# Router and expert stages joined into one block, norm rows loaded earlier, norm done in place, value read moved to the end

## The chip, the cores and the metric

The kernel runs on one core of a Trainium2 chip, as one program. The metric is the device time of one execution in microseconds, as the median over runs; smaller is better. The profile shows one execution of it, with the engines PE (TensorE), DVE (VectorE), ACT (ScalarE), POOL (GpSimd) and SP (SyncE), which only issues transfers here.

## The reference, cut to what matters

A sequence of 256 tokens of width 1024 goes through two layers of one transformer (attention mixers and a feed-forward net), and then through a second block, of which the end matters here: a layer norm, a router and 16 experts.

```python
def layer_norm(x, g, b):
    mu = jnp.mean(x, -1); var = jnp.mean(jnp.square(x - mu), -1)
    return (x - mu) * lax.rsqrt(var + LN_EPS) * g + b
...
# second block, after the mixer has added its output to x:
x = layer_norm(x, ln1_g, ln1_b)
scores = sigmoid(x @ w_router)                      # 16 experts, 4 groups of 4
biased = scores + router_bias
# of each group the best sum of two biased scores; the best group is kept;
# in it the two best experts; their scores, divided by their sum, are weights
x = ALPHA * x + sum over the chosen experts of
        weight * ((silu(x @ w_gate[e]) * (x @ w_up[e])) @ w_down[e])
return layer_norm(x, ln2_g, ln2_b)
```

(The lines under the dots are a summary in words of this text's own; the norm is the reference's, shortened.) Each token goes to two experts of one group.

## The kernel before, in words

Everything is in float32 precision. A float32 product is made of three products of a faster 32-bit form: the operand is split into a high part (ACT copies it, `Ring.hi`, L172) and a low part (DVE subtracts the high part from it, `Ring.lo`, L184), and PE multiplies high by high, high by low and low by high.

**Weights** come in units of 1 MB through a `Ring`: SP issues a unit's transfer (`Ring.feed`, L159) as soon as the raw slot of the unit five places earlier has been split by DVE; ACT and DVE split it into one of 4 pairs; PE multiplies by it and counts it as used, which lets ACT split the unit four places later. An expert has six units: two for the gate, two for the up product, two for the down product.

**Blocks.** The program is a row of blocks (`nc.Block()`): inside one, each engine has its own list of instructions, and the lists meet through semaphores only. At a block's end every engine stops until all are there. Around the change the order of blocks is:

1. `project("mixer_out", ...)` (L2782): the output products of the mixer, added to `x` by DVE (L2779). All its weight units are issued in the block before. Then `clear_semaphores` (L3516), a block of its own.
2. `normalize_and_route` (L2207, its block starts at L2225). SP issues the two norm rows (L2229, 512 KB each), router weights and bias (L2230, L2231), and the first five expert units. DVE sums `x` (L2166), then waits for the rows (`dve.wait_ge(*loaded)`), writes `(x - mean) * gain` into a work tile (L2170) and `work * rstd + bias` back into `x` (L2175). ACT squares (L2154) and POOL takes the inverse root (L259, L260) beside that. PE transposes `x` (L2244); ACT and DVE bring it to `hT` (L2274, L2299) and split `x` into the pair `x_pair` (L2276, L2302); PE multiplies by the router weights (L2254); ACT takes the sigmoid (L2279); DVE then works alone through small instructions of some 0.2 us, one waiting for the other: the group of each token (L2306 to L2318), then, after PE has counted the tokens of each group (L2259 to L2263), the slot of each token (`slot_key`, L2321), the **gather table** `G` of ones and zeros in eight instructions (L2325), the largest group (L2327), and the two experts' weights, `combine` (L2289 to L2337) and `combine_rest` (L2339).
3. `nc.values_load` (L2118): every engine reads the size of the largest group into a register.
4. `sparse_experts` (L2342, block at L2373). PE multiplies `x_pair` by the gather table, 16 pieces `n` of two 128x512 products (L2433), which sorts the tokens by group; the pieces go through 7 PSUM banks, and the even ones are taken out by ACT (L2475), the odd ones by DVE (L2477), two copies of 128x256 each. After pieces 2, 5, 10 and 13 PE turns one group's table (L2441) and gathers its weights (L2443), and ACT takes both out (L2492, L2493) after its pieces 2, 6, 10 and 14. ACT and DVE make the splits of units 0 to 3 between the pieces: unit 0 first of all, then one after ACT's pieces 4, 8, 12 and DVE's 5, 9, 13. When all is out, the experts run, 0 to 15: gate (L2385), turn of the expert before (L2396), up (L2385), down of the expert before (L2409), and after each fourth one the scatter back to tokens (L2423).
5. `nc.If(n_most > P)` (L2120 on): a dense path for the case in which a group has over 128 tokens. It isn't taken. Then `last_norm` with its own rows and work tile, and the result is stored.

`TileNorm` (L2143) is used by steps 2 and 5.

```python
PICK = (3, 6, 7, 4, 5, 0, 1)                      # banks of the gather's pieces
...
ring.lo(dve, 0)
for n in range(1, 16, 2):
    dve.wait_ge(picked, n + 1)
    picked_out(n)
    if n in (5, 9, 13):
        ring.lo(dve, n // 4)
```

## Time and profile before

| | |
|---|---|
| median of 3 runs | 1820.74 us (1813.05, 1820.74, 1821.1) |
| the profiled execution | 1813.24 us, of which the span of the trace is 1811.3 us |
| PE busy | 1604.7 us, 89% of the span |
| DVE busy | 1227.2 us, 68% |
| ACT busy | 816.4 us, 45% |
| moved by DMA | 348.07 MB, mean 192 GB/s |

Times in the rows are microseconds from the span's start. A row of the timeline gives start, length, engine, line and operation, how many instructions stand in it (x2: two, one behind the other), and in brackets the idle time ahead of it with what ended it. "PEq" and the like is the sequencer of an engine, which handles waits, branches and register loads.

### The profile page before, as it was taken

Reading aid. Unit: us, or ns where it says so; the run is one execution under the profiler, and the core shown is the slowest. Engines: PE = TensorE matmul, PEld = TensorE weight load, DVE = VectorE, ACT = ScalarE, POOL = GpSimd, SP = SyncE. Lnnn points to the kernel's source line nnn. Section 1 sums busy time; section 2 is a strip of 40 time slices with the busy share of each in tenths; the row PEclk is TensorE's granted clock in tenths of the full one; section 3 lists DMA queues with packets and bytes.
Section 4 is the critical chain, followed back from the end, with each engine's and each line's share of the span. In section 5 each row is a group of like instructions: output and inputs, shape, how many; then the busy total and the mean of one; then the engine's idle time right before and its main releaser. Section 6 shows DMA issues by size and latency. Waiting matters only on the chain. (4 is left out here: it accounts for less than half of the span.)

```text
span 1811.3 us, 25509 instructions
## 1 busy us (share of the span) xinstructions
PE 1604.7 (89%) x10701; PEld 1449.5 (80%) x10701; DVE 1227.2 (68%) x1354; ACT 816.4 (45%) x943; POOL 42.4 (2%) x60
## 2 busy tenths in 40 slices
PE   2899998999899998999969997897798958999995
PEld 2789887999798988899958997886686857888884
DVE  4877586988757557665554875534575757899895
ACT  1345533434344553443323662225433327777773
POOL 0100000000100000000000000000000000000000
PEclk9999999999999999999979998987887969999998
DMA  8975446999844324666245553111222447999992
GB/s 302 318 231 163 140 140 189 351 324 328 251 147 134 108 89 147 218 228 214 93 156 178 157 169 93 47 47 47 79 85 71 139 142 255 374 349 366 365 345 106
DMA packets 226057, 348.07 MB, mean 192 GB/s; under 512 B 14612, under 2 KB 156672, under 8 KB 225808
## 3 DMA queue, kind: packets, MB, share of 16 engines
q1 hardware_dynamic: 225936, 346.36, 57.1%
q8 instruction: 87, 1.43, 0.3%
q14 instruction: 34, 0.28, 0.1%
HBM read 345.29 MB, written 1.97 MB: 192 GB/s over the span
## 5 line engine op out<-in xcount | busy, mean ns | idle before, releaser
L459 PE MATMUL bank<-layer_split,hT_pair 128*128 128x256 f32 (+2 forms) x4032 | 512.7, 287 | 31.3 <-DVE hT_pair L1031 21.6
L459 PEld LDWEIGHTS bank<-layer_split,hT_pair 128*128 128x128 f32 x4032 | 486.2, 190 | 45.2 <-issue 29.9
L184 DVE TENSOR_TENSOR layer_split<-layer_raw,layer_split 128x2048 fp32r<-128x2048 f32 x122 | 279.6, 2292 | 100.8 <-ACT layer_split L172 99.4
L172 ACT ACTIVATE layer_split<-layer_raw 128x2048 fp32r<-128x2048 f32 x122 | 233.5, 1914 | 195.1 <-PE bank L459 73.7
L184 DVE TENSOR_TENSOR expert_split<-expert_raw,expert_split 128x2048 fp32r<-128x2048 f32 x96 | 219.5, 2290 | 40.7 <-ACT expert_split L172 40.6
L172 ACT ACTIVATE expert_split<-expert_raw 128x2048 fp32r<-128x2048 f32 x96 | 184.2, 1920 | 76.2 <-PE bank L2385 39.3
L459 PE MATMUL bank<-split_w,hT_pair 128*128 128x256 f32 (+1 forms) x1248 | 180.8, 308 | 13.6 <-PEq L2580 5.0
L459 PEld LDWEIGHTS bank<-split_w,hT_pair 128*128 128x128 f32 x1248 | 170.5, 204 | 24.3 <-issue 18.7
L184 DVE TENSOR_TENSOR split_w<-raw_w,split_w 128x2048 fp32r<-128x2048 f32 x52 | 119.2, 2293 | 66.2 <-ACT split_w L172 65.6
L1894 PE MATMUL bank<-layer_split,ffnh_aT 128*128 128x512 f32 x528 | 127.0, 396 | 2.8 <-DVE ffnh_aT L1962 2.8
L172 ACT ACTIVATE split_w<-raw_w 128x2048 fp32r<-128x2048 f32 x52 | 99.4, 1912 | 59.2 <-PE bank L459 50.7
L459 PE MATMUL bank<-hT_pair,split_w 128*128 128x256 f32 x960 | 120.7, 288 | 4.1 <-DVE hT_pair L315 4.0
L459 PEld LDWEIGHTS bank<-hT_pair,split_w 128*128 128x128 f32 x960 | 118.3, 193 | 5.7 <-issue 5.2
L1894 PEld LDWEIGHTS bank<-layer_split,ffnh_aT 128*128 128x128 f32 x528 | 98.0, 188 | 25.8 <-DVE ffnh_aT L1962 3.3
L2385 PE MATMUL bank<-expert_split,hT_pair 128*128 128x512 f32 x384 | 93.6, 401 | 4.2 <-DVE gathered_pair L2477 4.2
L2409 PE MATMUL bank<-expert_split,expert_hidden_T 128*128 128x512 f32 x384 | 91.3, 394 | 1.4 <-DVE expert_hidden_T L2543 1.4
L2385 PE MATMUL bank<-expert_split,gathered_pair 128*128 128x512 f32 x384 | 92.6, 396 | 0.0
L2385 PEld LDWEIGHTS bank<-expert_split,hT_pair 128*128 128x128 f32 x384 | 72.7, 191 | 21.2 <-issue 4.6
L2409 PEld LDWEIGHTS bank<-expert_split,expert_hidden_T 128*128 128x128 f32 x384 | 72.2, 188 | 18.0 <-DVE expert_hidden_T L2543 1.6
L2385 PEld LDWEIGHTS bank<-expert_split,gathered_pair 128*128 128x128 f32 x384 | 71.6, 188 | 16.3
L204 DVE SCALAR_TENSOR_TENSOR ada_acc<-layer_raw,silu_c,ada_acc 128x1024 f32<-128x1024 f32 x40 | 51.7, 1294 | 1.4
L459 PE MATMUL bank<-layer_split,merge_pair 128*128 128x256 f32 x384 | 47.8, 284 | 0.4 <-DVE merge_pair L1765 0.4
(455 smaller groups left out, 1756.4 us busy)
## 6 DMA issues: line engine op xcount, KB each, us to landing
layer_raw<-in_ada_w SPq DMA_DIRECT2D x48, 1024.0 KB, 6.9
layer_raw<-in_ffn_w_gate_up SPq DMA_DIRECT2D x44, 1024.0 KB, 5.6
raw_w<-in_w_in SPq DMA_DIRECT2D x40, 1024.0 KB, 5.1
layer_raw<-in_w_in SPq DMA_DIRECT2D x38, 1024.0 KB, 6.1
expert_raw<-in_w_gate SPq DMA_DIRECT2D x32, 1024.0 KB, 7.1
expert_raw<-in_w_up SPq DMA_DIRECT2D x32, 1024.0 KB, 7.2
expert_raw<-in_w_down SPq DMA_DIRECT2D x32, 1024.0 KB, 6.9
layer_raw<-in_ffn_w_down SPq DMA_DIRECT2D x22, 1024.0 KB, 5.4
```

What stands on the lines that cost most here:

```text
L172: self.nc.scalar.activation(self.pair[:, j % self.pairs, 0, 0:self.size[n]], self.raw[:, n % self.depth, 0:self.size[n]], ACT.Copy).then_i ...
L184: self.nc.vector.tensor_tensor(self.pair[:, j % self.pairs, 1, 0:self.size[n]], self.raw[:, n % self.depth, 0:self.size[n]], self.pair[:, ...
L204: self.nc.vector.scalar_tensor_tensor(acc[:, :], second, self.scale[:, 2 * q + 1:2 * q + 2], acc[:, :], ALU.mult, ALU.add).then_inc(self.l ...
L459: ins = nc.tensor.matmul(out, lhs, rhs, start=first and c == chunks[0] and tp + wp == 0, stop=last and c == chunks[-1] and tp == 1)
L1894: ins = nc.tensor.matmul(ps[4 + 2 * t + nb][:, :], self.aT[:, tp, c, t * P:(t + 1) * P], w[:, c, nb * 512:(nb + 1) * 512], start=n == 0 an ...
L2385: ins = nc.tensor.matmul(ps[bank][:, :], gathered[e // PER // 2][:, tp, 4 * i + c, slot_cut(e // PER)], ring.view(u + i, wp, 4, 512)[:, c, :],
L2409: ins = nc.tensor.matmul(ps[OUT_BANKS[nb]][:, :], aT[:, tp, 2 * i + c, :], ring.view(u + i, wp, 2, D)[:, c, nb * 512:(nb + 1) * 512], star ...
```

## The change

- The route step is no block of its own. `normalize_and_route` becomes `routing`, which returns four lists (tensor, scalar, vector, gpsimd), and `sparse_experts` becomes `routed_experts`, which puts them at the front of its own engines' lists, in its block.
- PE's gather waits for a semaphore `g_ready` of the eight table instructions. The weights `combine` have another, `combined`, which PE waits for ahead of the first table turned. The maximum (`most`) moves ahead of the slot key.
- The order in the gather changes: banks, who takes which piece out (ACT 9, DVE 7), where the tables stand (after pieces 6, 8, 10, 13), and the splits of units 0 to 3: ACT makes the high parts of 0, 1 and 2 behind the router's sigmoids and 3 behind the gather; DVE makes the low part of 0 while PE counts, 1 behind piece 7, and 2 and 3 behind the gather.
- Norm rows, router weights and bias are issued at the end of SP's list in the `mixer_out` block. The rows lie in `hT`, which is free there.
- The first norm writes `(x - mean) * gain` into `x` itself, and so waits for ACT's square of that tile first. The second norm keeps its work tile.
- `values_load` stands behind the experts' block, right ahead of the `If`.

```diff
+            def load_rows(sp):
+                rows, w, bias = ln_rows[0:3]
+                for i, name in enumerate(("ln1_g_2", "ln1_b_2")):
+                    sp.dma_start(rows[:, i, :], A[name].broadcast_to([P, D])).then_inc(rows_in, 16)
...
-                    normalize_and_route(ring, comb, member, key, rest, most, most_int, xP, G)
-                    n_most = nc.values_load(most_int[0:1, 0:1], min_val=0, max_val=S)
-                    sparse_experts(ring, comb, xP, G, s1)
+                    scratch = sb("silu_hidden", [P, D], s1)
+                    g_ready, combined = new_sem(nc, "route_tables_out"), Count(nc, "route_combined")
+                    route = routing(ring, comb, member, key, rest, most, most_int, xP, G, s1, ln_rows, scratch, g_ready, combined)
+                    routed_experts(ring, comb, xP, G, s1, scratch, route, g_ready, combined)
+                n_most = nc.values_load(most_int[0:1, 0:1], min_val=0, max_val=S)
...
                 dve.wait_ge(*loaded)
+                centred = x if self.in_place else self.work
                 for t in range(TILES):
-                    done(dve, v.scalar_tensor_tensor(self.work[:, t, :], x[:, t, :], rstat[:, t:t + 1], self.rows[:, 0, :],
+                    if self.in_place:
+                        dve.wait_ge(self.squared.sem, t + 1)
+                    done(dve, v.scalar_tensor_tensor(centred[:, t, :], x[:, t, :], rstat[:, t:t + 1], self.rows[:, 0, :],
...
+                ring.lo(dve, 0)
+                dve.wait_ge(counted, 1)
+                do(v.tensor_reduce(most[:, :], ps[6][:, 8:12], AX, ALU.max))
+                place = ps[6][:, 0:8].rearrange("p (t g) -> p t g", t=TILES)
+                do(v.scalar_tensor_tensor(key[:, :, :], place, 1.0, member[:, :, :], ALU.add, ALU.mult))
+                do(v.tensor_scalar(key[:, :, :], key[:, :, :], -1.0, None, ALU.add))
+                for t in range(TILES):
+                    for g in range(GROUPS):
+                        ins = v.tensor_scalar(G[:, t, g, :], const("slot"), key[:, t, g:g + 1], None, ALU.is_equal)
+                ins.then_inc(g_ready, 1)
...
-            PICK = (3, 6, 7, 4, 5, 0, 1)
+            PICK = (3, 7, 4, 5, 0, 6, 1)
+            BY_ACT = (0, 1, 2, 4, 6, 8, 10, 12, 14)
+            TABLES = (6, 8, 10, 13)
...
+                    route_tensor(pe)
+                    pe.wait_ge(g_ready, 1)
                     for n in range(16):
                         part, c = n // 8, n % 8
                         if n >= 7:
-                            m = n - 7
-                            pe.wait_ge(picked_act if m % 2 == 0 else picked_dve, m // 2 + 1)
+                            pe.wait_ge(*left(n - 7))
...
-                        if n in (2, 5, 10, 13):
-                            g = (2, 5, 10, 13).index(n)
+                        if n in TABLES:
+                            g = TABLES.index(n)
                             if g:
                                 pe.wait_ge(table_out, g)
+                            else:
+                                pe.wait_ge(combined.sem, 1)
...
-                    ring.hi(act, 0)
-                    for n in range(0, 16, 2):
+                    route_scalar(act)
+                    ring.hi(act, 2)
+                    for n in range(16):
...
-                        if n in (4, 8, 12):
-                            ring.hi(act, n // 4)
+                    ring.hi(act, 3)
...
-                    ring.lo(dve, 0)
-                    for n in range(1, 16, 2):
-                        dve.wait_ge(picked, n + 1)
-                        picked_out(n)
-                        if n in (5, 9, 13):
-                            ring.lo(dve, n // 4)
+                    route_vector(dve)
+                    for n in range(16):
+                        if n not in BY_ACT:
+                            dve.wait_ge(picked, n + 1)
+                            picked_out(n)
+                        if n == 7:
+                            ring.lo(dve, 1)
+                    ring.lo(dve, 3)
...
-                project("mixer_out", ring, jobs, banks=4, norm=OnlyTurn(ring, Turn("mixer_T", m, hP), U_OUT))
+                project("mixer_out", ring, jobs, banks=4, norm=OnlyTurn(ring, Turn("mixer_T", m, hP), U_OUT),
+                        extra={"sync": load_rows})
```

## Rows read from the trace of the kernel before

**Rows 1.** The page, part 5: the expert products, gate and up of half the experts.

```profile
L2385 PE MATMUL bank<-expert_split,hT_pair 128*128 128x512 f32 x384 | 93.6, 401 | 4.2 <-DVE gathered_pair L2477 4.2
```

**Rows 2.** Busy time by stretch: us, then PE, PEld, DVE, ACT, POOL, PEclk, DMA, GB/s.

```profile
1480.00:1490.00 10.00, 2.30 (x10) 2.21 (x10) 6.27 (x34) 0.08 (x1) 0.00 (x0) 0.50 0.00 0
1493.00:1494.00 1.00, 1.00 (x8) 0.96 (x7) 1.00 (x1) 0.78 (x4) 0.00 (x0) 0.77 0.00 0
1500.00:1504.00 4.00, 2.35 (x13) 1.40 (x11) 4.00 (x8) 4.00 (x10) 0.00 (x0) 0.96 0.74 252
1504.00:1510.00 6.00, 2.51 (x6) 2.06 (x7) 3.39 (x5) 0.71 (x4) 0.00 (x0) 0.50 0.89 286
1510.00:1511.00 1.00, 1.00 (x4) 0.79 (x4) 0.00 (x0) 0.00 (x0) 0.00 (x0) 0.73 1.00 410
1540.00:1560.00 20.00, 20.00 (x90) 16.18 (x89) 17.14 (x10) 14.41 (x9) 0.00 (x0) 1.00 1.00 383
```

**Rows 3.** Timeline of PE around the gather.

```profile
1490.04 2.90 PE L2433 MATMUL bank<-gather_table,x_pair 128*128 128x512 f32 x6 [7.65 <-PEq L2225]
...
1495.14 0.38 PE L2441 MATMUL bank<-cst,gather_table 128*128 128x128 f32 x2
...
1495.72 2.56 PE L2433 MATMUL bank<-gather_table,x_pair 128*128 128x512 f32 x10
...
1507.49 18.36 PE L2385 MATMUL bank<-expert_split,hT_pair 128*128 128x512 f32 x72 [4.15 <-DVE gathered_pair L2477]
```

**Rows 4.** Timeline of DVE, the first norm.

```profile
1466.28 2.60 DVE L2170 SCALAR_TENSOR_TENSOR ln_work<-x,rstat,ln_rows 128x1024 f32<-128x1024 f32 x2 [2.77 <-DMA ln_rows<-in_ln_b]
1468.92 2.61 DVE L2175 SCALAR_TENSOR_TENSOR x<-ln_work,rstat,ln_rows 128x1024 f32<-128x1024 f32 x2
```

**Rows 5.** Timeline of DVE, from the router to the first piece taken out.

```profile
1482.50 0.17 DVE L2321 SCALAR_TENSOR_TENSOR slot_key<-bank,group_member 128x8 f32<-128x8 f32 x1 [1.81 <-PE bank L2263]
...
1482.91 1.66 DVE L2325 TENSOR_SCALAR gather_table<-cst_second,slot_key 128x128 fp32r<-128x128 f32 x8
1484.60 0.16 DVE L2327 TENSOR_REDUCE most_tokens<-bank 128x1 f32<-128x4 f32 x1
...
1488.31 0.19 DVE L2337 TENSOR_TENSOR combine<-combine,router_max 128x32 f32<-128x32 f32 x1
...
1488.74 0.19 DVE L2339 TENSOR_TENSOR combine_rest<-combine,router_over 128x32 f32<-128x32 f32 x1
1491.86 2.29 DVE L184 TENSOR_TENSOR expert_split<-expert_raw,expert_split 128x2048 fp32r<-128x2048 f32 x1 [2.93 <-ACT expert_split L172]
1494.07 0.42 DVE L2477 CAST hT_pair<-bank 128x256 fp32r<-128x256 f32 x1
1494.40 0.42 DVE L2477 CAST gathered_pair<-bank 128x256 fp32r<-128x256 f32 x1
```

**Rows 6.** The sequencers' instructions of L2118, the value read.

```profile
L2118 DVEq TENSOR_LOAD <-most_tokens_int x1: 547/547/547, 1489.4 to 1489.4; - x1
```

**Rows 7.** Timeline of ACT: second square, second sigmoid, first split.

```profile
1463.60 1.15 ACT L2154 ACTIVATE ln_work<-x,rstat 128x1024 f32<-128x1024 f32 x1 [0.27 <-DVE rstat L2167]
1464.66 0.19 ACT L2154 ACTIVATION_READ_ACCUMULATOR ln_work<-x,rstat 128x1 f32 x1
...
1477.90 0.18 ACT L2279 ACTIVATE router_scores<-bank 128x16 f32<-128x16 f32 x1 [0.57 <-PE bank L2254]
1489.92 1.91 ACT L172 ACTIVATE expert_split<-expert_raw 128x2048 fp32r<-128x2048 f32 x1 [11.83 <-PEq L2225]
```

**Rows 8.** Transfers issued by SP.

```profile
1413.10 17.17 SPq L159 DMA_DIRECT2D raw_w<-in_w_out  x4
1460.61 0.34 SPq L2229 DMA_DIRECT2D ln_rows<-in_ln_g  x1
```

**Rows 9.** Timeline of POOL, the second inverse root.

```profile
1465.28 0.54 POOL L260 TENSOR_TENSOR rstat<-rstat,half_neg 128x1 f32<-128x1 f32 x1
```

**Rows 10.** Timeline of DVE at the end.

```profile
1799.60 1.22 DVE L2166 TENSOR_REDUCE rstat<-x 128x1 f32<-128x1024 f32 x1 [3.60 <-issue]
```

More of the change, by code:

```diff
@@ new lines, in routing, with gpsimd, tensor @@
+            squashed, step, member_out = (Count(nc, f"route_{n}") for n in ("squashed", "step", "member_out"))
+            norm = TileNorm("ln1", rows, None, 4.0 * LN_EPS, scratch[:, :])
+            def gpsimd(pool):
+                norm.gpsimd(pool)
+            def tensor(pe):
+                for t in range(TILES):
+                    pe.wait_ge(norm.normed.sem, t + 1)
+                    for k in range(KD):
+                        ins = nc.tensor.transpose(ps[k // 2][:, (k % 2) * S + t * P:(k % 2) * S + (t + 1) * P],
+                                                  x[:, t, k * P:(k + 1) * P], ident)
+                        if t == TILES - 1 and k % 2:
+                            ins.then_inc(turned, 1)
+                pe.wait_ge(router_in, 32)
+                for t in range(TILES):
+                    for k in range(KD):
+                        if t == 0 and k % 2 == 0:
+                            b = k // 2
+                            pe.wait_ge(dve_out if b % 2 else act_out, b // 2 + 1)
+                        ins = nc.tensor.matmul(ps[4 + t][:, 0:16], hT[:, k, t * P:(t + 1) * P], w[:, k, :],
+                                               start=k == 0, stop=k == KD - 1)
+                    ins.then_inc(scored, 1)
+                before = const("sb_strict")
+                pe.wait_ge(member_out.sem, 1)
+                nc.tensor.matmul(ps[6][:, 0:4], before, member[:, 0, :], start=True, stop=True)
+                nc.tensor.matmul(ps[6][:, 4:8], ones, member[:, 0, :], start=True, stop=False)
+                nc.tensor.matmul(ps[6][:, 4:8], before, member[:, 1, :], start=False, stop=True)
+                for t in range(TILES):
+                    ins = nc.tensor.matmul(ps[6][:, 8:12], ones, member[:, t, :], start=t == 0, stop=t == 1)
+                ins.then_inc(counted, 1)
@@ new lines, in bank_out, with scalar @@
+            def bank_out(b):
+                return hT[:, 2 * b:2 * b + 2, :].rearrange("p b s -> p (b s)"), ps[b][:, :]
+            def scalar(act):
+                norm.scalar(act)
+                for b in (0, 2):
+                    act.wait_ge(turned, b + 1)
+                    a.activation(*bank_out(b), ACT.Copy).then_inc(act_out, 1)
+                for t in range(TILES):
+                    a.activation(xP[:, 0, t, :], x[:, t, :], ACT.Copy).then_inc(x_hi, 1)
+                for t in range(TILES):
+                    act.wait_ge(scored, t + 1)
+                    signal(a.activation(sc[:, t, :], ps[4 + t][:, 0:16], ACT.Sigmoid), squashed)
@@ L2347, in sparse_experts, with routed_experts @@
+            return tensor, scalar, vector, gpsimd
+        def routed_experts(ring, comb, xP, G, st, scratch, route, g_ready, combined):
             v, a = nc.vector, nc.scalar
@@ L2371, in slot_cut, with left @@
                 return slice((g % 2) * P, (g % 2) * P + P)
+            def left(n):
+                by_act = sum(b <= n for b in BY_ACT)
+                return (picked_act, by_act) if n in BY_ACT else (picked_dve, n + 1 - by_act)
+            route_tensor, route_scalar, route_vector, route_gpsimd = route
             with nc.Block() as block:
@@ L2376, in _ @@
                     ring.feed(sp, len(ring.units))
+                @block.gpsimd
+                def _(pool):
+                    route_gpsimd(pool)
                 @block.tensor
```

217 lines of the change are left out of this document (79 added, 138 removed).

## The prediction

> **What bounds the kernel now.** I looked first at who is busy. PE is, 89% of the span, and in the 283 us of the experts it never stops: 20.00 us of 20 at the full granted clock [rows 2], and over the gate and up products of half the experts it was idle 4.2 us, all ahead of the first [rows 1]. So inside the experts nothing is to be had, and whatever lets the first expert product start earlier comes off the end one for one, as long as weights keep up. Then I read the timelines between the mixer's last product and that first one. Here PE is nearly idle and a chain of single steps sets the time. The reader should see five places in it. DVE waits 2.77 us for the norm rows, which SP issues only when this block begins [rows 4, 8]. DVE then works through the router and has the gather tables at 1484.57 (1482.91 and 1.66), but goes on to 1488.93 with weights that the gather doesn't need [rows 5]. PE starts the gather at 1490.04, held by the block's end and the value read behind it [rows 3, 6]. The gather takes until 1507.49 [rows 3], and DVE ends it, since four splits of 2.29 us stand among its pieces [rows 5]. And PE's clock is at its lower level, 1.2 GHz (0.50), for the first 3.4 us of the gather, and again from 1503.7, when PE had run short of work, to 1510.5 [rows 2].
>
> Everything below is summed against the profiled execution, 1813.24 us. The median is 1820.74 us, 7.5 us above it; two of the three runs lie there and one at 1813.05, so there are two levels between which the trace says nothing. I carry the difference over to the median.
>
> **Norm rows early, norm in place.** The rows are issued in the mixer's output block, whose own weights SP has asked for by 1430.3 [rows 8], so SP is free and the 2.77 us go. What is late next is ACT's square: DVE is free at 1463.51 (1466.28 less 2.77), ACT had the first tile's square at 1463.33 (1463.60 less its 0.27 of idling) and the second's at 1464.85 [rows 4, 7]. The first centring fits at 1463.55 and takes 1.30, so the second finds its square just done. The new wait costs 0 to 0.1, and everything behind shifts by **2.7 us**. The centring writes as many bytes to `x` as to the work tile: nothing. POOL's second inverse root is there at 1465.82 [rows 9], ahead of the end of both centrings at 1466.15. The rows' 1 MB could at most hold up the mixer's own weights by 2.6 us (at 410 GB/s, the best rate shown [rows 2]); the last of those was issued ahead of them, so I take 0. SP's four issues at the head of the block go as well, and the first five expert units start that much sooner; both kernels ask for five.
>
> **Low part of unit 0 while PE counts.** DVE reaches this point at 1480.69 (1482.50 less 1.81 of waiting) less 2.7, so 1477.95 [rows 5]. ACT is through its sigmoids at 1475.4 and has the high part at 1477.3 (1.91 [rows 7]); DVE's 2.29 end at 1480.25. PE's counts would be there at 1479.8 (1482.50 less 2.7). Then `most`, 0.20, now comes first. The slot key starts at 1480.45, so this pair of edits loses 0.65 us on the chain, and in return a whole split leaves the gather. From key to last table are 2.07 us [rows 5]: tables at **1482.5**. ACT's splits of units 1 and 2 end at 1481.1, before it has a piece to take out.
>
> **Gather behind its tables alone, no block change.** PE starts at 1482.6 in place of 1490.04: 7.4 us earlier, made of the 2.7, less 0.65, plus 4.36 of DVE's weights (1484.57 to 1488.93), plus about 1.1 of block end and read. What is late next is `combined`, on DVE 3.75 us after the tables (1484.57 to 1488.50, less 0.20 for `most`), so 1486.25. PE asks for it only after piece 6.
>
> **The gather itself.** PE is cold before it in both kernels [rows 2]. I take 3.4 us at the low clock as before, 0.43 to 0.45 a product, so 8 products, and then 0.256 (2.56 for 10 [rows 3]); the first 14 products end at 1487.5, so `combined` isn't waited for. Nine more pieces are 4.6 us and four tables 0.58 each, 2.3 (1495.14 to 1495.72): PE ends at 1494.5. DVE takes pieces out at 0.33 a copy [rows 5], some 0.75 a piece: 3 and 5 from 1486.7 (after `combine_rest`), 7 at 1489.4, its one split to 1491.7, then 9, 11, 13 and, when PE has it, 15 to 1495.3. ACT has nine pieces and four tables, about 8 us of work in 12. So the first expert product can start at **1495.3**, 12.2 us earlier: the gather stage is 12.7 us for 17.45. Splits 2 and 3 now end at 1499.9 and the up product that needs them starts at 1501.4; their cover is the 6 us of the gate product, and without it they would cost up to 4.6.
>
> **The clock.** The gap ahead of the first expert product shrinks from 4.15 us to under 1. Before, the products ran at the low level from 1507.49 to 1510.54 [rows 2, 3], which cost half of 3.05, so 1.5 us. No row shows a gap of 0.8 us after steady work. Bounds: 0 gain if it falls again, 1.5 if not. I take 1.5, because the fall at 1503.7 came after stop-and-go work (2.35 us busy in 4 [rows 2]), which this plan has not.
> The Trainium skill, "TensorE: Matmul & The Clock Gate", section "HAM oscillation", has it that a long idle gap lets the clock fall; by that alone the row at 1503.7, which fell 0.4 us after the last product, is not explained, so a short gap is no safe sign. By the row's reading the sum would lose the 1.5.
>
> **Value read at the end.** It leaves the chain at 1489.4 (counted above) and comes back ahead of the branch, where all engines stand: 0.55 us, DVE's own [rows 6]. It lies behind the last addition with nothing beside it. The idle 3.60 us ahead of the last norm's first instruction [rows 10] is there in both. Lower bound 0, upper 0.55 plus another such wait, 3.6; I take 0.55, the row of the same instruction.
> "Runtime: NRT & Kernel Launch", section "Instruction fetch mechanics", of the Trainium skill gives about 0.2 us for a register loaded from HBM and says that a taken branch stalls the fetch: with 0.2 the sum would be 13.4 in place of 13.2. The 547 ns here are from on-chip memory and decide; the stall agrees with the 3.60 and speaks against putting anything ahead of that branch.
>
> **Sum.** 12.2 and 1.5, less 0.55: 13.2 us. 1813.24 becomes 1800.0 at the lower level, and the median 1820.74 becomes **1807.5**. Differences under 0.5%, 9.1 us, are what a measurement of this kernel can't tell from none.
>
> **Rivals.**
> - *The clock stays low through the gather.* If the short router products leave PE colder, 18 later products and the tables cost another 4 us, and the first expert starts low: gain 13.2 less 4 less 1.5, 7.7, time 1813. For it: 1480 to 1490 at 0.50 throughout [rows 2]. Against: in both starts that are shown the clock rose within 3.5 us. 0.12.
> - *ACT and DVE bound the gather.* If DVE's last four pieces, all behind its split, take 1.5 us each for 0.75, that is 3 us more and a gap in which the clock falls as well: gain 8.7 to 10.2, time 1811. For it: pieces queue behind one 2.29 us split. Against: PE delivers only each 1.1 us. 0.12.
> - *A second fetch stall at the branch.* Gain 13.2 less 3.6, 9.6, time 1811. Against: the read sits in a straight list. 0.06.
> - *Weights can't follow.* DMA engines are 1.00 busy at 383 GB/s [rows 2]. Only units 0 to 4 are brought forward fully; unit 6 is asked for at 1491.7 and needed at 1513, so this could cost 0 to 3 us. Against: 410 GB/s is possible and PE never waited. 0.03.
> - *Slower: the lower clock holds on into the experts.* Place: from the gather's start, where PE goes on after 3 us of idling. Each microsecond of products at 1.2 GHz costs 0.5 us, so it cancels the gain after 26 us of them; 50 us would give 1819, or slower than before by 0.5% from 45 us on. Against: low stretches under load last 3.4 us at most in the rows. 0.03.
> The Trainium skill's clock page, section "Seeing it yourself", warns that the clock has been seen stuck low for over 50 us; no run here shows it.
> - *The edit does little,* because something unseen (a transfer, code) holds the gather's start: gain under 5. 0.03.
>
> **How the numbers follow.** The forecast (gain 11 to 15) has 0.61. The range adds both levels: 1820.74 less 8.7 is 1812, with 1.5 for rivals at its edge, 1813.5; the lower level less 15 is 1798. So 1798 to 1813.5; no more than 2 in 10 is outside. Faster by over 0.5% are the forecast, the branch stall and half to two thirds of the two gather rivals, with a bit off and on for the two levels: 0.79. Within: 0.17. Slower: 0.04.
>
> **What would show it.** In the changed profile: no DMA wait ahead of the first centring; DVE at the slot key 2.0 us earlier; PE's first gather product 7.4 us earlier; 12.7 us from it to the first expert product; that product at full clock; a register load of 0.5 us ahead of the branch. The prediction is wrong if PE waits in the gather for `combined` or a bank, if a gap over 2 us stands ahead of the experts, or if the experts' PE shows waits.

## The result, and the profile after

| | before | after |
|---|---|---|
| median (runs) | 1816.88 us (7, 1813.05 to 1821.1) | 1797.32 us (7, 1796.16 to 1806.0) |
| ratio of the runs | | 0.9899, 95% interval 0.9878 to 0.9921 |
| the profiled execution | 1813.24 us, span 1811.3 | 1797.32 us, span 1795.4 |
| mean granted clock | 0.946 | 0.950 |

The kernel is faster, by 1.0%: 18.4 us by the ratio (14.4 to 22.2), 19.6 by the medians. The forecast was 1807.5 us, its range 1798 to 1813.5, from a median of 1820.74 us over three runs. On that start the ratio gives 1802.4 us, inside the range; the measured median itself, 1797.32, lies 0.7 us below it, since the median of the kernel before is 1816.88 over seven runs. The direction holds, but the gain is over the forecast's 13.2 us and over its "gain 11 to 15". The profiled pair differs by 15.9 us.

First what the expert products waited for, on the page of the kernel after, part 5; it answers to [rows 1]:

```profile
L2399 PE MATMUL bank<-expert_split,hT_pair 128*128 128x512 f32 x384 | 92.5, 397 | 0.9 <-ACT gathered_pair L2492 0.9
```

The idle time ahead of them fell from 4.2 us to 0.9. The norm and the router, timeline of DVE, after (start, length, instruction; in brackets the idle time before it), as in [rows 4, 5]:

```profile
1455.84 0.42 DVE L2799 SCALAR_TENSOR_TENSOR x<-x,bank 128x256 f32<-128x256 f32 x1 [2.30 <-PE bank L459]
...
1460.30 2.71 DVE L2188 SCALAR_TENSOR_TENSOR x<-x,rstat,hT 128x1024 f32<-128x1024 f32 x2
1463.04 1.28 DVE L2193 SCALAR_TENSOR_TENSOR x<-x,rstat,hT 128x1024 f32<-128x1024 f32 x1
1464.82 1.28 DVE L2193 SCALAR_TENSOR_TENSOR x<-x,rstat,hT 128x1024 f32<-128x1024 f32 x1 [0.49 <-POOL rstat L260]
...
1474.76 2.29 DVE L184 TENSOR_TENSOR expert_split<-expert_raw,expert_split 128x2048 fp32r<-128x2048 f32 x1
1476.97 0.15 DVE L2321 TENSOR_REDUCE most_tokens<-bank 128x1 f32<-128x4 f32 x1
1477.16 0.17 DVE L2323 SCALAR_TENSOR_TENSOR slot_key<-bank,group_member 128x8 f32<-128x8 f32 x1
1477.36 0.17 DVE L2324 TENSOR_SCALAR slot_key<-slot_key 128x8 f32<-128x8 f32 x1
1477.56 1.66 DVE L2327 TENSOR_SCALAR gather_table<-cst_second,slot_key 128x128 fp32r<-128x128 f32 x8
```

The reader should see the missing bracket on the first centring (L2188): no wait for the rows. In [rows 4] it had 2.77 us there. There is a smaller wait further on, 0.49 us for POOL's inverse root. The split of unit 0 (L184) stands ahead of `most` and the slot key, where DVE used to wait for PE's counts, and the tables end at 1479.22.

POOL's timeline, after, answers to [rows 9]:

```profile
1463.14 1.59 POOL L260 TENSOR_TENSOR rstat<-rstat,half_neg 128x1 f32<-128x1 f32 x1
```

The same instruction took 0.54 us before, when DVE was waiting beside it; now DVE works through 1024-wide rows at that time. POOL's two operations ahead of it grew too (0.54 to 1.52 and 0.19 to 0.99 us).

The rows came early enough. SP's issues in the kernel after (its timeline), as in [rows 8]:

```profile
1410.86 17.16 SPq L159 DMA_DIRECT2D raw_w<-in_w_out  x4
1430.87 0.34 SPq L2109 DMA_DIRECT2D hT<-in_ln_g  x1
```

The gather, timeline of PE, after, as in [rows 3]:

```profile
1479.28 5.86 PE L2448 MATMUL bank<-gather_table,x_pair 128*128 128x512 f32 x14 [2.85 <-DVE gather_table L2327]
1484.97 0.38 PE L2458 MATMUL bank<-cst,gather_table 128*128 128x128 f32 x2
...
1490.83 1.19 PE L2448 MATMUL bank<-gather_table,x_pair 128*128 128x512 f32 x4
1492.92 1.40 PE L2399 MATMUL bank<-expert_split,hT_pair 128*128 128x512 f32 x5 [0.89 <-ACT gathered_pair L2492]
```

The row names ACT for the last wait, but ACT's last copy ended at 1492.25; what ended right ahead of the first expert product is DVE's copy of the last piece, in DVE's timeline:

```profile
1492.40 0.41 DVE L2494 CAST gathered_pair<-bank 128x256 fp32r<-128x256 f32 x1
```

PE starts when the tables are there (the gather's first product names DVE's table, no longer the sequencer) and runs to the last piece with no wait. It asks for `combine` at 1484.97; DVE wrote it at 1482.84. The granted clock in that stretch (the windows view: us, then PE, PEld, DVE, ACT, POOL, PEclk, DMA, GB/s), as in [rows 2]:

```profile
1483.00:1484.00 1.00, 1.00 (x4) 0.81 (x3) 0.93 (x4) 0.06 (x1) 0.00 (x0) 0.50 0.00 0
1484.00:1485.00 1.00, 1.00 (x5) 0.73 (x5) 0.36 (x2) 0.60 (x2) 0.00 (x0) 0.79 0.00 0
1486.00:1492.00 6.00, 6.00 (x36) 4.74 (x34) 4.94 (x9) 3.72 (x15) 0.00 (x0) 1.00 0.22 46
1492.00:1494.00 2.00, 1.11 (x6) 0.94 (x6) 1.94 (x3) 2.00 (x2) 0.00 (x0) 1.00 0.99 385
```

Two things are to be seen. The clock is at 1.2 GHz (0.50) until about 1484.4, so for 5.1 us from the gather's start and not 3.4; and it is full at the first expert product, over the gap of 0.89 us. The end, timeline of DVE, after, as in [rows 10]:

```profile
1783.67 1.22 DVE L2181 TENSOR_REDUCE rstat<-x 128x1 f32<-128x1024 f32 x1 [4.31 <-issue]
...
1787.13 2.60 DVE L2188 SCALAR_TENSOR_TENSOR ln_work<-x,rstat,ln_rows 128x1024 f32<-128x1024 f32 x2 [0.61 <-DMA ln_rows<-in_ln_b]
```

And the sequencers' instructions of L2133, the value read, after, as in [rows 6]:

```profile
L2133 DVEq TENSOR_LOAD <-most_tokens_int x1: 550/550/550, 1779.7 to 1779.7; - x1
```

The whole by stage, from these rows and their like in both traces:

| stage, its end | before | after | difference | forecast |
|---|---|---|---|---|
| to the mixer's last addition (DVE) | 1459.08 | 1455.84 | -3.24 | 0 |
| to the first centring | 7.20 | 4.46 | -2.74 | -2.7 |
| to the slot key | 16.22 | 16.86 | +0.64 | +0.65 |
| to the gather's first product | 7.54 | 2.12 | -5.42 | -5.35 |
| to the first expert product | 17.45 | 13.64 | -3.81 | -4.8 |
| to the last additions (DVE) | 285.83 | 283.95 | -1.88 | -1.5 |
| to the last norm's first instruction | 6.28 | 6.80 | +0.52 | +0.55 |

Behind the mixer's last addition these make -12.7 us, for -13.2 forecast (the forecast's column makes -13.15; one part of it was rounded). The other 3.2 us lie ahead of the norm, where of the change's own instructions only SP's four early issues stand. Where the medians' further microseconds lie, no trace of this pair can tell.

### The profile page after: what moved, and what is told of

Same layout as the page of the kernel before. It is cut to its first block and busy times, and to the rows that moved or that the text cites. A ratio compares the mean times of both kernels' runs of the same rounds, so it can differ in the third digit from the quotient of the medians.

```text
span 1795.4 us, 25499 instructions
## 1 busy us (share of the span) xinstructions
PE 1597.9 (89%) x10701; PEld 1443.7 (80%) x10701; DVE 1225.5 (68%) x1352; ACT 817.2 (46%) x945; POOL 43.9 (2%) x60
## 5 line engine op out<-in xcount | busy, mean ns | idle before, releaser
L184 DVE TENSOR_TENSOR layer_split<-layer_raw,layer_split 128x2048 fp32r<-128x2048 f32 x122 | 279.6, 2292 | 101.6 <-ACT layer_split L172 99.9
L184 DVE TENSOR_TENSOR expert_split<-expert_raw,expert_split 128x2048 fp32r<-128x2048 f32 x96 | 219.1, 2289 | 30.4 <-ACT expert_split L172 30.2
L459 PE MATMUL bank<-split_w,hT_pair 128*128 128x256 f32 (+1 forms) x1248 | 173.2, 301 | 14.9 <-PEq L2600 5.0
L459 PEld LDWEIGHTS bank<-split_w,hT_pair 128*128 128x128 f32 x1248 | 163.1, 201 | 25.7 <-issue 17.1
L184 DVE TENSOR_TENSOR split_w<-raw_w,split_w 128x2048 fp32r<-128x2048 f32 x52 | 119.2, 2292 | 64.2 <-ACT split_w L172 63.6
L1929 ACT ACTIVATE ffnh_aT<-bank 128x512 fp32r<-128x512 f32 x22 | 13.1, 597 | 80.0 <-PE bank L1882 80.0
```

The costliest lines, as they stand in the source:

```text
L184: self.nc.vector.tensor_tensor(self.pair[:, j % self.pairs, 1, 0:self.size[n]], self.raw[:, n % self.depth, 0:self.size[n]], self.pair[:, ...
L459: ins = nc.tensor.matmul(out, lhs, rhs, start=first and c == chunks[0] and tp + wp == 0, stop=last and c == chunks[-1] and tp == 1)
L1929: nc.scalar.activation(self.aT[:, 0, :, :].rearrange(flat), ps[2][:, :], ACT.Copy).then_inc(self.hi_out, 1)
```

## The experiments

Each ratio is to runs of the kernel before on the same chip. "From the last addition" is the time from the mixer's last addition to the first expert product in the trace: 48.41 us before, 37.08 after.

### The kernel after once more

> The changed kernel once more, unchanged, against before. The traces account for 12.7 us of gain behind the mixer's last addition, and another 3.2 us lie ahead of it, where the code is the same. Theory A (that part is how this kernel varies from one execution to the next): the ratio comes out with an interval that holds 0.9930 (12.7 us), and this trace differs from the first one of the same kernel by 1 us or more ahead of the mixer's last addition. Theory B (the change speeds up earlier stages too, by another layout of memory or code): the ratio is again 0.990, and every trace of the changed kernel has its mixer's last addition over 2 us ahead of every trace of before.

1797.3 us (1789.22 to 1800.99, 6 runs), ratio 0.9877 (0.9855 to 0.99). From the last addition 37.14 us; the gather took 13.94. So the whole of it repeats to 0.1 us and single stages to 0.3; the gather's first 14 products took 6.15 us here. But the last addition came at 1452.67, another 3.2 us earlier, in the same kernel. Neither theory came out whole: the interval doesn't hold 0.9930, as A wanted, and the last addition varies by 3.2 us with the code unchanged, which B doesn't explain.

### The kernel before once more

> The kernel before, unchanged, against itself. It tells what two groups of runs of one program differ by: the ratio should hold 1.0 within 0.25%. Of 26 runs of it in the last call most took 1815 to 1823 us at a mean granted clock of 0.941 to 0.947 and the rest 1800 to 1811 us at 0.948 to 0.954, and the traces so far come from the second kind (1813 us at 0.946, and 1810 and 1808 us for its two relatives). If this trace is of the first kind, I expect its 4 to 8 us more ahead of the norm, between 1070 and 1370 us, where the clock is not at its full level throughout, and the stretch from the mixer's last addition to the end as in the trace of before, within 0.5 us. Rival: the more lies in the experts, or is spread evenly.

1817.66 us (1807.7 to 1820.9, 12 runs), ratio 0.9979 (0.9961 to 0.9996). An interval that just leaves 1 out, for the same program: single results here are good to some 0.2%, 4 us, whatever the interval says. The trace, span 1818.1, has the last addition at 1462.92, 3.8 us later than the first trace of before, and from the last addition 51.65 us in place of 48.41. I had expected that stretch within 0.5 us. Of the 3.2 us more, 2.7 are in the router. Timeline of PE, the kernel before again:

```profile
1477.83 6.85 PE L2254 MATMUL bank<-router_w,hT 128*128 128x16 f32 x32
```

In the first traces of before and after these 32 products took 4.37 and 4.21 us, since the clock was full for their first 3 us; here it was low throughout (0.50 from 1467 to 1492). One program thus has executions that differ by 3 us in this stage and by 4 ahead of it. It is not this kernel's alone: of the 14 traces four have this row at 6.84 or 6.85 us (this one, the old order, the 64 bytes more and the kernel without a branch) and ten at 3.75 to 4.37. The times of those four from the last addition can't be set against 37.08 without taking some 2.7 to 2.9 us off.

### The rows early, and nothing else

Edit, on the kernel before: what the change does for SP (rows in `hT`, router weights ahead of the mixer's tiles), with the norm's work tile, the blocks and the order kept.

```diff
+                project("mixer_out", ring, jobs, banks=4, norm=OnlyTurn(ring, Turn("mixer_T", m, hP), U_OUT),
+                        extra={"sync": load_rows})
```

> The kernel before with one part of the change: the norm rows, router weights and bias are issued in the mixer's output block; the norm keeps its work tile. My theory: only the wait of 2.77 us for the rows goes, nothing is late in its place, so the first centring starts 0.1 us behind the means and the first expert product comes 2.7 us sooner after the mixer's last addition (48.0 us behind that addition's start at 1459.08 before drops from 48.4 to 45.7). Whole time: 2.7 us less, which 3 rounds can hardly tell. Rival (the rows' transfer holds up the mixer's own weights): a wait of 1 to 2.6 us appears in the output products and the gain is near 0.

1807.16 us (1801.31 to 1808.35, 4 runs), ratio 0.9925 (0.9901 to 0.9949): 13.6 us. Timeline of DVE, rows early:

```profile
1460.92 2.61 DVE L2182 SCALAR_TENSOR_TENSOR ln_work<-x,rstat,hT 128x1024 f32<-128x1024 f32 x2
```

No wait, and from the last addition 45.74 us: -2.67, the 2.7 of the first step. The total is five times that, so something ahead of the norm had changed. It shows in the mixer's output products, 192 in one row of PE's timeline. The kernel before, then this one:

```profile
1435.95 23.02 PE L459 MATMUL bank<-split_w,hT_pair 128*128 128x256 f32 x192 [0.85 <-DVE hT_pair L315]
```

```profile
1434.34 22.02 PE L459 MATMUL bank<-split_w,hT_pair 128*128 128x256 f32 x192 [0.85 <-DVE hT_pair L315]
```

The same products, both with the clock full, 1.0 us apart; the kernel after has 22.02 too. An earlier row of 192 such products, at 1021 us, shows the same step, 23.39 us before and 22.12 after. What the edit and the change have in common is that `router_w` (512 bytes a partition) and `router_bias` (64) are allocated ahead of the mixer's weight tiles, which therefore lie 576 bytes further on.

### Shifting the weight tiles alone

Edit, on the kernel before: a tile that nothing uses, of 576 bytes a partition, and of 512 in the second kernel (`[P, 128]`).

```diff
             with ExitStack() as st:
+                sb("pad", [P, 144], st)
                 ring = Ring(nc, "second", sb("raw_w", [P, 3, UNIT], st), sb("split_w", [P, 2, 2, UNIT], st, FR), units)
```

> The kernel before with one thing more: an unused tile of 576 bytes per partition ahead of the mixer's weight tiles, which is what the changed kernel's router weights and bias put there (they move the raw and the split tile from 63744 and 88320 to 64320 and 88896). Theory B2 (the place of the weight tiles in memory sets PE's pace in the mixer; all four traces with the move need 22.02 us for the 192 output products, both without it 23.02): 22.02 us here, the same step at 1018 to 1031 us (10.83 us between two DVE instructions for 11.9 to 13.1), nothing at the norm or behind, and a whole time 2 to 6 us below before. Rival A (it comes from the rows' early transfer, or from chance): 23.02 us and no difference in the whole.

> The same with 512 bytes in place of 576: the weight tiles move almost as far, but stay at a multiple of 256 bytes, as before. Theory B2 in its narrow form (the place within 256 or 128 bytes counts): 23.02 us for the 192 output products and the time of before. In its wide form (how far the tiles lie from the tokens' pair, or in which bank): 22.02 us, like the 576.

576 bytes: 1809.41 us (1805.96 to 1812.19, 12 runs), ratio 0.9961 (0.9933 to 0.9988). 512 bytes: 1817.05 (1804.55 to 1822.44, 10 runs), ratio 0.9988 (0.9966 to 1.0011). The output products, timeline of PE, with 576 and then with 512:

```profile
1435.33 22.02 PE L459 MATMUL bank<-split_w,hT_pair 128*128 128x256 f32 x192 [0.85 <-DVE hT_pair L315]
```

```profile
1430.60 23.03 PE L459 MATMUL bank<-split_w,hT_pair 128*128 128x256 f32 x192 [0.85 <-DVE hT_pair L315]
```

So an unused tile sets the pace of these products, and 576 does what 512 doesn't. Behind the norm nothing moved (from the last addition 48.86 with 576). Its gain in time, 7.1 us by the ratio and 7.6 against the 512 kernel, has the size of what the change gained beyond the forecast's steps; but the two intervals overlap, and one program against itself gave 0.9979, so the totals support it and don't show it. By the rows the pace is worth less: 1.0 us in these products and 1.0 to 1.3 in the row at 1021 us, some 2.2.

### The kernel after with the tiles shifted by 64 bytes more

```diff
+                sb("pad", [P, 16], st)
```

> The changed kernel with an unused tile of 64 bytes per partition ahead of the mixer's weight tiles, so that they lie at a multiple of 128 bytes again (64384 for 64320). If the place within 128 bytes sets PE's pace in the mixer (113 ns a product at 64320, 120 at 63744 and 64256), the 192 products at 1018 us take 23.4 us for 22.1 and the output products 23.0 for 22.0, the mean clock falls towards that of before, and the median lies 4 to 10 us above the changed kernel's 1797.3; all behind the mixer as in the changed kernel. If the place within 256 bytes sets it (64384 is not a multiple of 256), nothing changes: 22.1, 22.0 and 1797.

The pace went back: timeline of PE, the kernel after with 64 bytes more:

```profile
1429.94 23.27 PE L459 MATMUL bank<-split_w,hT_pair 128*128 128x256 f32 x192 [0.85 <-DVE hT_pair L315]
```

The row at 1021 us went back as well, to 23.38. The time did not: 1797.27 us (1796.18 to 1798.81, 5 runs), ratio 0.9875 (0.9855 to 0.9896). The totals here can't tell 2 us from none, so this leaves a pace worth 2 us standing, and it forbids the simple account "the layout gained 7 us by the pace". From the last addition the trace has 39.85 us, with the slow router row. Ahead of the norm it makes some of this good in a stretch of the recurrences, between the same two products by their place in PE's list: 50.0 us here (from 1291.9), 53.0 before (from 1293.0). It needs no change of address: the kernel with the read late, whose tiles lie as before, has 49.9 us there, and the repeat of the kernel after 51.1, for 52.9 in its first trace.

### The value read at the end, alone

```diff
                     normalize_and_route(ring, comb, member, key, rest, most, most_int, xP, G)
-                    n_most = nc.values_load(most_int[0:1, 0:1], min_val=0, max_val=S)
                     sparse_experts(ring, comb, xP, G, s1)
+                n_most = nc.values_load(most_int[0:1, 0:1], min_val=0, max_val=S)
```

> The kernel before with one part of the change: the value read stands behind the experts' block. My theory: it saves 0.55 us between the two blocks and costs 0.55 to 0.75 us at the end (the changed kernel had 4.31 us of idling ahead of the last norm for 3.60), so the whole is within 0.5 us of before. Rival (a read there makes the fetch behind the branch later by a stall of its own): 3 us or more are added at the end, and idling ahead of the last norm is over 6 us.

1817.99 us (10 runs), ratio 1.0006 (0.9986 to 1.0025): nothing, as it should be. PE's wait ahead of the gather, 7.65 us in [rows 3], is 7.06 here; the idle time at the end is 3.99 for 3.60. So 0.6 us taken from one place is mostly paid at the other. No second stall came with it.

### The gather waits for the weights

Edit, on the kernel after:

```diff
                     pe.wait_ge(g_ready, 1)
+                    pe.wait_ge(combined.sem, 1)
```

> The changed kernel, with PE's gather waiting for the weights as well as for the tables. My theory (DVE's 3.75 us of weights were on the chain): the gather's first product starts 3.4 us later; PE is as cold as before, so the gather stage itself gets 1 us shorter at most since pieces 3 and 5 no longer wait for DVE; the first expert product 2.5 to 3.5 us later than in the changed kernel. Rival (the gather's end is set by DVE and ACT, and an early start is lost in waiting): under 1 us later.

1802.37 us (4 runs), ratio 0.992 (0.9896 to 0.9945). Timeline of PE, this kernel:

```profile
1482.15 5.63 PE L2449 MATMUL bank<-gather_table,x_pair 128*128 128x512 f32 x14 [6.57 <-DVE combine L2338]
...
1495.52 1.87 PE L2399 MATMUL bank<-expert_split,hT_pair 128*128 128x512 f32 x7 [0.90 <-ACT gathered_pair L2493]
```

From the last addition 40.58 us, 3.5 more than after. That is what the gather's start "behind its tables alone" is worth: the gather starts 3.7 us later, the length of DVE's weights, and its stage is 0.3 us shorter.

### The old order of pieces and splits

Edit, on the kernel after: banks, shares and the splits of units 1 to 3 as before; the low part of unit 0 and the places of the tables stay.

```diff
-            PICK = (3, 7, 4, 5, 0, 6, 1)
-            BY_ACT = (0, 1, 2, 4, 6, 8, 10, 12, 14)
+            PICK = (3, 6, 7, 4, 5, 0, 1)
+            BY_ACT = (0, 2, 4, 6, 8, 10, 12, 14)
...
-                        if n == 7:
-                            ring.lo(dve, 1)
-                    ring.lo(dve, 3)
+                        if n in (5, 9, 13):
+                            ring.lo(dve, n // 4)
```

> The changed kernel with the old order within the gather: banks as before, even pieces to ACT and odd ones to DVE, high parts of units 1 to 3 behind ACT's tables and low parts behind DVE's pieces 5, 9 and 13 (unit 0's stay ahead, the table turns stay behind pieces 6, 8, 10 and 13). My theory (DVE's splits among its pieces end the gather): the start of the gather is as in the changed kernel, its length grows from 13.6 by 3 to 5 us, since ACT's four and DVE's three splits stand in it, and a gap of over 2 us ahead of the first expert product brings the lower clock back. Rival (PE's cold start sets the gather): under 1 us longer.

1804.32 us (7 runs), ratio 0.993 (0.9906 to 0.9955). Timeline of PE, then the windows view, this kernel:

```profile
1476.80 5.82 PE L2448 MATMUL bank<-gather_table,x_pair 128*128 128x512 f32 x14 [2.85 <-DVE gather_table L2327]
...
1494.56 5.73 PE L2399 MATMUL bank<-expert_split,hT_pair 128*128 128x512 f32 x15 [3.86 <-DVE gathered_pair L2494]
```

```profile
1494.00:1498.00 4.00, 3.44 (x8) 2.80 (x9) 0.45 (x2) 0.00 (x0) 0.00 (x0) 0.50 0.94 337
1498.00:1500.00 2.00, 2.00 (x8) 1.53 (x8) 0.00 (x0) 0.32 (x1) 0.00 (x0) 0.76 0.08 33
```

The gather takes 17.76 us for 13.64, with DVE's splits among its pieces again, and the gap of 3.86 us brings the low clock back into the experts, which then take 285.96 us to the last additions for 283.95. So the order of the pieces is worth 4.1 us and, through the clock, 2.0 more. It doesn't carry the early start: with the old order the gather takes as long as in the kernels with the old blocks, which start it late (17.45 us before, 17.5 to 18.1 in their other five traces), so PE doesn't wait longer for having started early, and the two gains add up.

### PE kept busy

Edit, on the kernel after: idle products into an unused bank, 26 ahead of the transposes, 8 behind the router products, 10 behind the counts. They compute nothing that is used.

```diff
+            def keep_warm(n):
+                for _ in range(n):
+                    nc.tensor.matmul(ps[7][:, :], hP[:, 0, 0, 0:P], hP[:, 0, 0:2, :].rearrange("p c s -> p (c s)"),
+                                     start=True, stop=True)
```

> The changed kernel with products that compute nothing needed, on PE alone, into a bank that is free: 26 of 128x512 while DVE does the norm, 8 while it takes the first steps of the router, 10 while it makes the tables. They test the clock term. My theory: the 16 transposes take 2 us for 3.4, the gather starts at the full clock or reaches it within 2 us, and it takes 11.0 to 12.0 us for 13.6; together 3 to 4 us sooner from the mixer's last addition to the first expert product. Rival (the short products of the router bring the clock down whatever stands around them, or the extra products make DVE's releases wait): the gather starts at 0.50 as before, and the gain is under 1.5 us, all from the transposes.

> The changed kernel with 44 idle products once more, with more rounds, to see whether the 2.75 us that the trace showed from the mixer's last addition to the first expert product (34.3 us for 37.1) are in the measured time: the same 34.3 us within 0.3, and a median 2 to 4 us under the changed kernel's 1797.3. Rival: the extra products are paid back elsewhere, and the median is that of the changed kernel.

1794.0 us (1791.7 to 1799.14, 4 runs), ratio 0.9881 (0.9843 to 0.9918), and again 1793.48 (1788.67 to 1796.88, 5 runs), 0.9849 (0.9825 to 0.9872). Timeline of PE, the first of the two:

```profile
1453.77 6.16 PE L2244 MATMUL bank<-hT_pair 128*128 128x512 f32 x26 [1.68 <-PEq L3545]
...
1463.80 3.78 PE L2262 MATMUL bank<-router_w,hT 128*128 128x16 f32 x32 [0.19 <-ACT hT L2283]
1467.41 3.61 PE L2244 MATMUL bank<-hT_pair 128*128 128x512 f32 x8
...
1474.95 3.47 PE L2456 MATMUL bank<-gather_table,x_pair 128*128 128x512 f32 x14 [0.52 <-DVE gather_table L2335]
...
1486.53 1.64 PE L2407 MATMUL bank<-expert_split,hT_pair 128*128 128x512 f32 x6 [0.89 <-DVE gathered_pair L2502]
```

The gather's first 14 products take 3.47 us for 5.86, and from the last addition it is 34.34 us, then 34.45 in the repeat: -2.7 and -2.6 from 37.08, a little under the 3 to 4 that I expected. Of it 2.1 us are in the gather's stage (11.58 for 13.64), which was thus lost to the clock and to no engine. The rest is ahead of the slot key: the 16 transposes are through in 2.9 us for 3.4, not in 2. The totals settle nothing: the ratios of the kernel after are 0.9899 and 0.9877, and these are 0.9881 and 0.9849, with intervals that overlap those of the 0.9877. By the medians it is 3.3 and 3.8 us faster. This step stands on the traces.

### No branch

Edit, on the kernel after: the value read, the branch and the dense path are left out. These inputs don't take that path.

```diff
-                n_most = nc.values_load(most_int[0:1, 0:1], min_val=0, max_val=S)
-
-                with nc.If(n_most > P):
...
```

> The changed kernel without the value read, the branch and the dense path behind it, which these inputs don't take. It prices the end. My theory: the idling ahead of the last norm's first instruction, 4.1 to 4.3 us in the changed kernel, falls to about the 1.15 us that an ordinary change of two blocks costs elsewhere or less, because the read's 0.55 us and the fetch at the jump's target both go: 3.0 to 3.5 us less, of which some is given back by a wait for the last norm's rows, which are issued there. Rival (the idling is the block change itself): under 1 us less.

1793.72 us (1790.58 to 1807.82, 5 runs), ratio 0.9852 (0.9827 to 0.9877); the profiled execution is the longest of the five. Timeline of DVE, this kernel, at the end:

```profile
1789.57 2.48 DVE L2537 TENSOR_TENSOR x<-x,bank 128x512 f32<-128x512 f32 x4 [0.83 <-PE bank L2427]
1792.37 1.22 DVE L2171 TENSOR_REDUCE rstat<-x 128x1 f32<-128x1024 f32 x1 [0.32 <-PEq L2373]
...
1797.72 2.60 DVE L2178 SCALAR_TENSOR_TENSOR ln_work<-x,rstat,ln_rows 128x1024 f32<-128x1024 f32 x2 [2.51 <-DMA ln_rows<-in_ln_b]
```

The time between the last additions' start and the norm is 2.80 us for 6.80, so the read and the branch cost 4.0 us together, more than the 3.0 to 3.5 that I expected, and the block's change isn't what cost them; but 1.9 of these come back, since the norm now waits 2.51 us for its rows (0.61 after). The stall of [rows 10] hid a load. The Trainium skill, "Runtime: NRT & Kernel Launch", section "Instruction fetch mechanics", says that a taken branch whose target isn't in the instruction buffer stalls its engine; the trace agrees in that the idle time goes with the branch, and puts the price here, with the read of 0.5, at 4.0 us. That the fetch is what takes it, no run here shows.

## Why the prediction was right, and where it was not

The steps behind the mixer's last addition came out, -12.7 us for -13.2. The total didn't come from them alone: some 6 us of it were in no term, and that it lies inside the range on the old start owes to the room that the range left for two levels of the median. That part is luck.

- **Rows early: right.** -2.74 between the traces, -2.67 alone, for 2.7. The in-place centring cost 2.71 for 2.60 us in two instructions, 0.1, at the upper end of "0 to 0.1". One statement failed: POOL's second root was not ahead of the end of both centrings (1463.01) but at 1464.73, because POOL's operations took 1.52, 0.99 and 1.59 us for 0.54, 0.19 and 0.54. The 0.49 us of waiting were made up until the split of unit 0, which DVE began 14.46 us behind the first centring; before, it stood waiting for PE's counts from 14.41 us on.
- **Low part while PE counts: right.** Forecast 0.65 on the chain, measured 0.64.
- **Gather behind its tables: right.** The gather's start is 7.52 us earlier from the last addition (the second to fourth differences), for 7.4. `combine` was 2.1 us ahead of PE's asking. Putting the wait back cost 3.5.
- **The gather itself: the mis-sized term.** "I take 3.4 us at the low clock as before, 0.43 to 0.45 a product, so 8 products": it was 5.1 us, and 6.15 us for the first 14 products in the repeat. So the stage took 13.64 (13.94) for 12.7, and the first expert product came 11.33 us earlier and not 12.2. The price of one row had been carried over. That row was the shortest of its kind: in the other five traces of the old blocks the clock was low for 3.6 to 4.8 us from the gather's first product, and in the six of the joined block without idle products, for 4.7 to 5.8. The rival in which the clock stays low through the gather was nearer than the forecast said by 1.7 us (2.4 in the repeat), but no more: the clock was full for the last 8 us. Kept busy, the stage took 11.6.
- **ACT and DVE as the bound: not so,** but for DVE's copy of the last piece, which ends the stage as forecast (0.9 us behind PE for 0.8). The old order shows what it would have cost, 4.1 us.
- **The clock into the experts: right.** The gap of 0.89 us left it at full level; the experts' stage gained 1.88 us for 1.5. The trace doesn't decide between the forecast's two readings: a short gap behind steady work is harmless by both. In the old order the clock fell 1.4 us into the gap of 3.86, behind work with gaps of 0.7 us at most, and it pays 2.0; a long gap alone may do.
- **Read at the end: right.** +0.52 for 0.55 (+0.28 in the repeat), nothing in sum when moved alone, no second stall. Not foreseen was what was late next: the second norm's rows, 0.61 us behind the stall.
- **What was missing.** The sum looked for effects of the early rows on the queue, on memory traffic and on the norm, and had none for the address of tiles that the edit doesn't name. The output products took 22.02 us for 23.02, the 192 earlier ones at 1021 us 22.12 for 23.39 (23.13 in the repeat of before). That is 2.0 to 2.3 us of pace. The shift alone measured 7.1 us, with an interval from 2.2 to 12.2.
- **Two slips in the working.** In the rival of a clock that stays low into the experts, 50 us at half a microsecond each are 25, and 1807.5 becomes 1832.5, not 1819. With 0.2 us for the read the sum is 13.5, not 13.4. Neither bears on the forecast.

**What stays open.** Beyond the 12.7 us the medians gained some 6 more. That it comes with the shift of 576 bytes is supported by the two kernels with an unused tile, and by the early rows alone, which gained 13.6 for 2.7 of their own; it isn't shown, since the interval of the shift alone begins 2.2 us from nothing and one program against itself came out at 0.9979. That the products' pace is the full cause is refuted by the rows, which hold 2.0 to 2.3 us of it, and by the 64 bytes more. In 14 traces the last addition stands between 1450.5 and 1465.8, with a mean of 1457.7 in the four with the tiles at the old or the 512-byte place and 1455.5 in the ten others: the scatter of one execution is larger than the effect, and more of it is in the recurrences than in the 1000 us ahead of them; there the mean clock from 1070 to 1370 us is 0.85 to 0.90 of full, by the execution. Telling the shares apart needs many more profiles than were taken.

## What to carry to other kernels

When a serial stage ahead of a long PE-bound one is shortened, follow the chain to each engine's next wait: here the start behind the tables was worth 3.5 us, and the new order of the pieces 4.1 and through the clock 2.0 more, each by itself. Keeping the tensor engine multiplying through a serial stretch, with products that nobody reads, took 2.7 us off it in two traces; the totals don't settle it. Price a low clock from more than one row. And when an edit moves an allocation, run the old kernel with an unused tile of that size beside it, or the layout's share will be booked as the edit's.

## What the runs showed of the hardware that was not expected

- **An operand's place in on-chip memory changes the pace of 128x256 products at full clock.** 192 of them took 22.0 us (115 ns each) or 23.0 to 23.3 (120 to 121), and the same choice held in every repeat of a kernel: 23.0 in four traces with the tiles at the old place or 512 bytes further, 22.0 in seven with 576, 23.27 in the one with 640. Two kernels with 576, the old order of the gather and the one without a branch, had 22.85, though their 192 products at 1021 us took 22.12 like the others', so the address isn't the only condition.
- **The clock fell on a busy engine.** With idle products ahead of them, the 32 router products (128x16) ran from 1463.80 to 1467.58, with PE busy 4.3 us of the 5 up to 1467, and yet the clock was down at 1467.3, among the last of them. In the first traces it fell among them too, at 1476.4 before and 1470.8 after. Windows view, PE kept busy:

```profile
1462.00:1467.00 5.00, 4.30 (x37) 4.09 (x38) 3.60 (x5) 3.93 (x5) 0.00 (x0) 1.00 1.04 392
1467.00:1471.00 4.00, 4.00 (x16) 3.29 (x15) 3.29 (x15) 3.90 (x5) 0.00 (x0) 0.57 0.68 247
1471.00:1486.00 15.00, 13.98 (x77) 11.01 (x75) 13.81 (x45) 9.65 (x29) 0.00 (x0) 1.00 0.30 87
```

  The longest idle gap between the first idle product (1453.77) and that fall was 0.8 us. The Trainium skill, "TensorE: Matmul & The Clock Gate", section "HAM oscillation", explains falls by long waits between products; this fall had none ahead of it, so that is not the only cause.
- **The clock stayed low under steady work.** In the kernel before once more PE went from the transposes into the router products with no gap, 10.3 us in all, and the clock didn't rise:

```profile
1475.00:1484.00 9.00, 9.00 (x45) 9.00 (x43) 4.46 (x5) 4.55 (x6) 0.00 (x0) 0.50 0.96 375
```

  In the first trace of the same kernel it rose 2.7 us behind the first transpose (1470.26 to 1473.0). So one trace doesn't price a stage of short products.
- **A small POOL operation slows by a factor of three beside wide DVE work.** The product on one number a partition took 0.54 or 0.55 us in all five traces in which DVE was waiting for the rows, and 1.52 to 1.59 in all nine in which the rows were early and DVE ran 128x1024 beside it. It put 0.49 us on DVE's chain.
